# Delta stage: a level's transposes and the next level's first product put into one step

## The chip, the cores and the metric

One core of one Trainium2 chip runs the kernel. The metric is the device time of one execution in microseconds (us). A figure for a kernel is the median of several executions. Besides these, one execution was taken by the hardware profiler. Its span, from the first to the last instruction, and its own rows are what the argument below works with. TensorE multiplies matrices, VectorE (DVE in the rows), ScalarE (ACT) and GpSimd (POOL) do the element-wise work, and SyncE (SP) issues the DMAs.

## The reference, cut to what matters

The model has two layers. The first has a gated delta rule as its mixer, the second an attention. The change touches the delta rule alone, here for one head, with chunks of 64 tokens:

```
L = where(strict, (k*beta) @ k.T * decay, 0)            # per chunk, 64 x 64
u, w = solve(I + L, [v*beta, k*beta*exp(g)])            # unit lower triangular
for each chunk:
    v_new = u - w @ state
    o     = (q*exp(g)) @ state + a_qk @ v_new
    state = state * exp(g_last) + (k*exp(g_last - g)).T @ v_new
o = rms_norm(o, norm_g) * silu(z)
```

q, k, v and z come from a projection of the input (1024 tokens by 1024 features), a causal convolution with four taps and a SiLU; q and k are normalized. There are 8 heads of 128 columns.

## The kernel before, in words

`delta_net` runs 9 iterations (`it` = 0 to 8) of 64 steps (`s` = 0 to 63). The order of all work is written out by hand: every engine has a loop over the same steps and does in each step what is placed there, in order, and semaphores alone tie the engines together. An engine that reaches a step early goes on until a wait holds it.

In iteration `it` TensorE projects head `it`: each step has three matmuls of 128x512 columns (`project`, L424 to L426). Behind the three come the pieces of the head before, `p = it - 1` (`head_work`). So iterations 1 to 7 have both, iteration 0 has no head work, and iteration 8 has no projection; there `keep_warm` (L465) issues one dummy matmul in each step from `AT_CHUNKS` on.

The pieces of head work on TensorE, in order of steps before the change:

- step 1 and 2: the products k k (L486) and k q (L490); step 3, 8 and 9: transposes (`turn`, L475) of k, of the first inverse `inv` and of v.
- steps 11 to 28, the levels: `(I + L)` is inverted by doubling blocks in 6 levels of three steps. The first step of a level is the product y (L526, in the last level L522), which DVE masks (L848, L844). The second is the product x (L546, L541), which DVE adds into `inv_t` (L861, L857). The third has the four transposes of `inv_t` (L475), which ACT copies to `inv` (L717). The last level has no transposes, so step 28 is empty.
- steps 29 to 52, the chunks: 8 pairs of chunks of three steps each, one for each matmul that waits for DVE: L560 waits for the state (L873), L566 for the rest (L866), L570 for v_new (L870).
- step 59: the column sums of the squared output (`column_sums`, L470, here "the second sums").

Head `it` has work of its own in the same iteration, at fixed steps: DVE convolves it in the odd steps from 9 to 55 (`convolve`, L787 for the first tap and L789 for the others; six half tensors of four taps). ACT takes each projected half out of PSUM in every eighth step (L620, L613), applies SiLU at step 41 (up to L660), and TensorE makes the column sums of the squared k at step 45 (L470, "the first sums"). ACT turns those into a norm (L645 to L649). Then come, on ACT, the half of step 48 (L620), the squares of q (L668, step 51), the high part of the next weights (L604, step 52), the second half of the output (L728) and its square (L729, step 53). On POOL come the normalization of k (L402, step 49), the low part of those weights (L391, step 52) and the sum of the two squares of the output (L405, step 53), for which the second sums wait. At step 59 ACT turns the second sums into a norm, DVE applies it (L831, step 62) and goes on to the next head's triangular matrix and its first inverse (L814 to L825), for which the transposes of step 8 wait. In iteration 7 there are no more weights to split, so L604 and L391 of step 52 are absent.

`keep_warm` and the wait of the second sums look like this:

```
rounds = int(s >= AT_CHUNKS)
...
pe.wait_ge(norms, p + 2)
pe.wait_ge(o_added, p + 1)
column_sums((w0[:, 0:HALF], w0[:, HALF:T]), eg, o_summed)
```

Of the kernel before, what the change touches and what calls it, by code (L numbers as in the profile page):

```python
# [15 lines left out]
NT = T // P  # L16
# [8 lines left out]
LEVELS = 6  # L25
# [202 lines left out]
AT_FIRST = 8  # L228
AT_VALUES = 9
AT_LEVELS = 11  # L230
AT_CHUNKS = 29
AT_O_TAKE = 41
AT_SILU = 41
AT_K_SUMS = 45
# [15 lines left out]
def delta_net(nc, c, ring, ahead, after, xh, xl, gates, w_in, gate_bias, a_log_dram, conv_w, norm_g, g_rows_dram, qkvz_space, o_t):  # L250
    with Phase(nc, "gdn") as ph:
# [8 lines left out]
        inv, inv_t = sb("inv", [P, T // 2]), sb("inv_t", [P, T // 2])  # L260
# [22 lines left out]
        w0, w1, w2 = ps("w0", [P, T]), ps("w1", [P, T]), ps("w2", [P, T])  # L283
# [13 lines left out]
        k_turned, kd_made = sem("k_turned"), sem("kd_made")  # L297
        kk_made, qk_made, att_made = sem("kk_made"), sem("qk_made"), sem("att_made")
        q_decayed, inv2_made, inv2_turned, inv2_copied = sem("q_decayed"), sem("inv2_made"), sem("inv2_turned"), sem("inv2_copied")
        y_product, y_made, x_product, x_made = sem("y_product"), sem("y_made"), sem("x_product"), sem("x_made")  # L300
        t_turned, t_copied = sem("t_turned"), sem("t_copied")
# [112 lines left out]
        def _(pe):  # L414
# [58 lines left out]
            def turn(out, src, signal, chunks):  # L473
                for n in chunks:
                    mm = pe.transpose(out[:, chunk(n)], src[:, chunk(n)], c["ident"][:])  # L475
                mm.then_inc(signal, 1)

            def head_work(p, s):
                q, k, v = (qkvz[:, p % 2, n] for n in range(3))
                if s == AT_KK:  # L480
                    pe.wait_ge(normed, p + 1)
                    if p:

                        pe.wait_ge(s_made, 9 * p)
                    for n in range(NT):
                        mm = pe.matmul(w2[:, chunk(n)], k[:, chunk(n)], k[:, chunk(n)], start=True, stop=True)  # L486
                    mm.then_inc(kk_made, 1)
                if s == AT_QK:
                    for n in range(NT):
                        mm = pe.matmul(w1[:, chunk(n)], k[:, chunk(n)], q[:, chunk(n)], start=True, stop=True)  # L490
                    mm.then_inc(qk_made, 1)
                if s == AT_FIRST:
                    pe.wait_ge(inv2_made, p + 1)
                    turn(w2, inv, inv2_turned, range(NT // 2))
                if s == AT_KEYS:
                    if p:

                        pe.wait_ge(o_rms, p)
                    turn(w0, k, k_turned, range(NT))
                if s == AT_VALUES:  # L500
                    pe.wait_ge(v_ready, p + 1)
                    pe.wait_ge(att_made, p + 1)
                    turn(w1, v, v_turned, range(NT))
                if s == AT_O_SUMS:
                    if p + 1 < H:

                        pe.wait_ge(norms, p + 2)
                    pe.wait_ge(o_added, p + 1)
                    column_sums((w0[:, 0:HALF], w0[:, HALF:T]), eg, o_summed)
                level, what = (s - AT_LEVELS) // 3, (s - AT_LEVELS) % 3  # L510
                if 0 <= level < LEVELS:
                    last = level == LEVELS - 1
                    if what == 0:
                        if level == 0:
                            pe.wait_ge(inv2_copied, p + 1)
                        else:
                            pe.wait_ge(x_made, LEVELS * p + level)
                        for q2 in range(NT // 2):
                            for m in range(2):
                                n = 2 * q2 + m  # L520
                                if last:
                                    mm = pe.matmul(w2[side(m), place(1, q2, HALF_P)], lower[side(1), own(n, 0)],  # L522
                                                   inv_t[side(1), square(n)], start=True, stop=True)
                                    continue
                                for b in (m, 1 - m):
                                    mm = pe.matmul(as_blocks(w2[side(m), place(b, q2, HALF_P // 2)], level),  # L526
                                                   lower[side(b), own(n, b)],
                                                   right_halves(inv_t[side(b), square(n)], level),
                                                   start=True, stop=True)
                        mm.then_inc(y_product, 1)  # L530
                    if what == 1:
                        pe.wait_ge(y_made, LEVELS * p + level + 1)
                        if level == 0:

                            pe.wait_ge(bv_made, p + 1)
                        else:
                            pe.wait_ge(t_copied, (LEVELS - 1) * p + level)
                        for q2 in range(NT // 2):
                            for m in range(2):
                                if last:  # L540
                                    mm = pe.matmul(w1[side(0), place(m, q2, HALF_P)], inv[side(m), square(2 * q2)],  # L541
                                                   y[side(m), square(q2)], start=True, stop=True)
                                    continue
                                for b in (m, 1 - m):
                                    at = (b * NT // 2 + q2) * HALF_P // 2
                                    mm = pe.matmul(w1[side(b), place(m, q2, HALF_P // 2)], inv[side(m), square(2 * q2 + b)],  # L546
                                                   y[side(m), at:at + HALF_P // 2], start=True, stop=True)
                        mm.then_inc(x_product, 1)
                    if what == 2 and not last:
                        pe.wait_ge(x_made, LEVELS * p + level + 1)  # L550
                        if level == 0:

                            pe.wait_ge(kd_made, p + 1)
                        turn(w0, inv_t, t_turned, range(NT // 2))
                n, what = (s - AT_CHUNKS) // 3, (s - AT_CHUNKS) % 3
                if 0 <= n < NT and s >= AT_CHUNKS:
                    if what == 0:
                        pe.wait_ge(s_made, 9 * p + n + 1)
                        pe.wait_ge(q_decayed, p + 1)
                        pe.matmul(w2[:, 0:P], k[:, chunk(n)], state[:, n % 2], start=True, stop=True).then_inc(ks_made, 1)  # L560
                        pe.matmul(w0[:, chunk(n)], state[:, n % 2], q[:, chunk(n)], start=True, stop=False)
                    if what == 1:
                        pe.wait_ge(x_made, LEVELS * (p + 1))
                        pe.wait_ge(full_made, 2 * p + 2)
                        pe.wait_ge(rest_made, NT * p + n + 1)
                        pe.matmul(w2[:, HALF:HALF + P], full_t[:, chunk(n)], rest[:], start=True, stop=True  # L566
                                  ).then_inc(tr_made, 1)
                    if what == 2:
                        pe.wait_ge(vn_made, NT * p + n + 1)
                        pe.matmul(w1[:, 0:P], k_rows[:, chunk(n)], v_new[:], start=True, stop=True).then_inc(ds_made, 1)  # L570
                        pe.matmul(w0[:, chunk(n)], v_new[:], att_t[:, chunk(n)], start=False, stop=True
                                  ).then_inc(o_made, 1)
# [20 lines left out]
        def _(act):  # L593
# [89 lines left out]
            for it in range(H + 1):  # L683
                p = it - 1
                for s in range(STEPS):
# [22 lines left out]
                    if s == AT_VALUES:  # L708
                        act.wait_ge(v_turned, p + 1)
                        for n in range(NT):  # L710
                            step(act.activation(v_rows[:, chunk(n)], w1[:, chunk(n)], ACT.Copy,
                                                scale=gates["beta"][:, n, p:p + 1]),
                                 bv_made, n == NT - 1)
                    level, what = (s - AT_LEVELS) // 3, (s - AT_LEVELS) % 3
                    if 0 <= level < LEVELS - 1 and what == 2:
                        act.wait_ge(t_turned, (LEVELS - 1) * p + level + 1)
                        step(act.activation(inv[:], w0[:, 0:HALF], ACT.Copy), t_copied)  # L717
                        if level == LEVELS - 2:
                            act.wait_ge(x_made, LEVELS * p + LEVELS - 1)
                            for b in range(2):  # L720
                                step(act.activation(full_t[side(b)].rearrange("p (n two t) -> p n two t", n=NT, two=2)[:, :, b],
                                                    inv_t[side(b)].rearrange("p (n t) -> p n t", n=NT), ACT.Copy), full_made)
# [15 lines left out]
        def _(dve):  # L738
# [69 lines left out]
            def head_work(p, s):  # L808
# [24 lines left out]
                if s == AT_QK:  # L833
# [1 line left out]
                    dve.wait_ge(decays, 2 * p + 2)  # L835
                    step(dve.tensor_tensor(att_t[:, 0:HALF], w1[:, 0:HALF], att_t[:, 0:HALF], ALU.mult))
                    step(dve.tensor_tensor(att_t[:, HALF:T], w1[:, HALF:T], att_t[:, HALF:T], ALU.mult), att_made)
                level, what = (s - AT_LEVELS) // 3, (s - AT_LEVELS) % 3
                if 0 <= level < LEVELS:
                    last = level == LEVELS - 1  # L840
                    if what == 0:
# [1249 lines left out]
```

## Time and profile before

| | us |
|---|---|
| median of 3 executions | 1914.57 |
| lowest, highest | 1911.27, 1914.67 |
| profiled execution, its own time | 1915.8 |
| profiled execution, span | 1912.1 |
| busy in the span: PE, DVE, ACT, POOL | 1770.5, 927.3, 755.9, 238.5 |
| delta stage in the span, about | from 25 to 719 |
| mean granted TensorE clock | 0.973 |

The table is to be read with care for TensorE: its matmuls are pipelined and the ends of them are modelled, so that two matmuls overlap in the rows and a busy engine need not be one at its peak. In the sums below, distances between starts are used wherever that is possible. POOL's share is small, but its single instructions are long.

### The profile page before, as it was taken

The numbers are of one execution on the slowest core, as the hardware profiler recorded it, in microseconds if no ns is written. First come the engines' busy times: TensorE is split into PE (matmuls) and PEld (weight loads), VectorE is DVE, ScalarE is ACT, GpSimd is POOL, SyncE is SP. The second block draws the span as 40 slices with busy tenths as digits, with TensorE's granted clock in tenths as the row PEclk, the third lists the DMA queues.
The fourth block names the chain that finished last, engine by engine and source line by source line (L and its number), as shares of the span: only waits on it lengthen the run. The fifth ranks groups of instructions, "written<-read, shape, count | busy, mean of one in ns | idle before, by whom it ended". The sixth has DMA issues, their size and how long they took to land. (4 is left out here: it accounts for less than half of the span.)

```text
span 1912.1 us, 29101 instructions
## 1 busy us (share of the span) xinstructions
PE 1770.5 (93%) x11308; PEld 1307.7 (68%) x11308; DVE 927.3 (48%) x1748; ACT 755.9 (40%) x1239; POOL 238.5 (12%) x199
## 2 busy tenths in 40 slices
PE   7999999999999779979989999999999999899798
PEld 5777777777777648768777886555555555478587
DVE  3767677676675627553322101334334443465523
ACT  3536455354553514042223213545544554441411
POOL 2212212122121101200000001111111110012000
PEclk9999999999999889989989999999999999989899
DMA  5111011210111005141031102111111101041311
GB/s 135 41 51 34 23 46 19 49 35 23 46 31 37 1 1 166 34 132 42 36 101 45 46 0 56 42 28 39 29 42 28 37 19 39 1 158 40 97 56 47
DMA packets 113799, 92.34 MB, mean 48 GB/s; under 512 B 19776, under 2 KB 95744, under 8 KB 113664
## 3 DMA queue, kind: packets, MB, share of 16 engines
q1 hardware_dynamic: 113664, 90.49, 16.4%
q8 instruction: 90, 1.47, 0.3%
q14 instruction: 45, 0.37, 0.1%
HBM read 81.99 MB, written 8.49 MB: 47 GB/s over the span
## 5 line engine op out<-in xcount | busy, mean ns | idle before, releaser
L424 PE MATMUL gdn_unit<-part_hi,gdn_w_hi 128*128 128x512 f32 x512 | 235.4, 460 | 0.2 <-DVE gdn_w_lo L746 0.2
L426 PE MATMUL gdn_unit<-part_hi,gdn_w_lo 128*128 128x512 f32 x512 | 201.7, 394 | 0.0
L425 PE MATMUL gdn_unit<-part_lo,gdn_w_hi 128*128 128x512 f32 x512 | 200.7, 392 | 0.0
L1954 DVE CUSTOM_DVE_ANT_0 fa_probs<-fa_scores,fa_decay 128x896 f32<-128x896 f32 (+7 forms) x128 | 97.0, 758 | 125.0 <-PE fa_scores L1769 80.5
L1788 PE MATMUL fa_turned<-ident,fa_probs 128*128 128x128 f32 x576 | 102.9, 288 | 32.8 <-ACT fa_probs_t L1903 15.4
L1788 PEld LDWEIGHTS fa_turned<-ident,fa_probs 128*128 128x128 f32 x576 | 61.0, 140 | 104.5 <-issue 52.3
L789 DVE SCALAR_TENSOR_TENSOR x<-gdn_raw,gdn_taps,x 128x512 f32<-128x512 f32 x144 | 123.7, 859 | 5.1
L1903 ACT ACTIVATE fa_probs_t<-fa_turned 128x512 f32<-128x512 f32 (+1 forms) x96 | 52.3, 545 | 181.7 <-PE fa_turned L1788 180.8
L1721 PE MATMUL fa_unit<-part_hi,fa_w_hi 128*128 128x512 f32 x256 | 115.0, 449 | 1.5 <-DVE fa_w_lo L1981 1.5
L426 PEld LDWEIGHTS gdn_unit<-part_hi,gdn_w_lo 128*128 128x128 f32 x512 | 96.1, 188 | 21.5
L1961 DVE COPY fa_probs_t<-fa_turned 128x512 f32<-128x512 f32 (+3 forms) x96 | 47.2, 491 | 127.2 <-PE fa_turned L1788 126.9
L391 POOL TENSOR_TENSOR gdn_w_lo<-ring,gdn_w_hi 128x1024 fp32r<-128x1024 f32 x31 | 75.2, 2424 | 269.0 <-ACT gdn_w_hi L604 269.0
L1897 ACT ACTIVATE fa_probs<-fa_probs,fa_top 128x896 f32<-128x896 f32 (+7 forms) x128 | 99.6, 778 | 20.0 <-DVE fa_top L1954 16.0
L424 PEld LDWEIGHTS gdn_unit<-part_hi,gdn_w_hi 128*128 128x128 f32 x512 | 96.9, 189 | 15.0 <-issue 3.6
L1186 PE MATMUL e_gate<-e_w_hi,e_a_hi 128*128 128x512 f32 x256 | 103.1, 403 | 2.8 <-DVE e_a_lo L1323 2.8
L425 PEld LDWEIGHTS gdn_unit<-part_lo,gdn_w_hi 128*128 128x128 f32 x512 | 97.3, 190 | 10.9 <-issue 3.6
L1723 PE MATMUL fa_unit<-part_hi,fa_w_lo 128*128 128x512 f32 x256 | 101.0, 394 | 0.0
L953 PE MATMUL m_y<-part_hi,m_o_hi 128*128 128x512 f32 x256 | 100.6, 393 | 0.0
L954 PE MATMUL m_y<-part_lo,m_o_hi 128*128 128x512 f32 x256 | 100.2, 391 | 0.0
L1188 PE MATMUL e_gate<-e_w_hi,e_a_lo 128*128 128x512 f32 x256 | 100.1, 391 | 0.0
L955 PE MATMUL m_y<-part_hi,m_o_lo 128*128 128x512 f32 x256 | 100.0, 391 | 0.0
L1722 PE MATMUL fa_unit<-part_lo,fa_w_hi 128*128 128x512 f32 x256 | 100.0, 391 | 0.0
(290 smaller groups left out, 3616.3 us busy)
## 6 DMA issues: line engine op xcount, KB each, us to landing
ring<-in_gdn_w_in_dram SPq DMA_DIRECT2D x32, 512.0 KB, 4.1
ring<-in_ple_w_gate_dram SPq DMA_DIRECT2D x32, 256.0 KB, 3.0
ring<-in_fox_w_in_dram SPq DMA_DIRECT2D x32, 256.0 KB, 3.2
ring<-in_fox_w_in_dram SPq DMA_DIRECT2D x16, 512.0 KB, 4.8
fa_decay<-c_rows_scratch SPq DMA_DIRECT2D x64, 128.0 KB, 3.1
in_x_tile<-in_x_dram SPq DMA_DIRECT2D x8, 512.0 KB, 6.7
gdn_g_bc<-g_rows_scratch SPq DMA_DIRECT2D x8, 512.0 KB, 8.5
m_old<-in_x_dram SPq DMA_DIRECT2D x8, 512.0 KB, 3.6
```

What stands on the lines that cost most here:

```text
L424: pe.matmul(out, w_hi[:, j % 2, k, :], xh[:, k, ts], start=(k == 0), stop=False)
L425: pe.matmul(out, w_hi[:, j % 2, k, :], xl[:, k, ts], start=False, stop=False)
L426: mm = pe.matmul(out, w_lo[:, j % 2, k, :], xh[:, k, ts], start=False, stop=(k == KT - 1))
L789: step(dve.scalar_tensor_tensor(out, shifted, weight, out, ALU.mult, ALU.add), conv_made if part == TAPS - 1 else None)
L953: pe.matmul(y[:, cols], o_hi[:, t % OB, k, :], w_hi[:, k, cols], start=(k == 0), stop=False)
L954: pe.matmul(y[:, cols], o_hi[:, t % OB, k, :], w_lo[:, k, cols], start=False, stop=False)
L955: mm = pe.matmul(y[:, cols], o_lo[:, t % OB, k, :], w_hi[:, k, cols], start=False, stop=(k == KT - 1))
L1186: pe.matmul(out[:, cols], hi, w_hi[:, k, cols], start=first, stop=False)
L1188: mm = pe.matmul(out[:, cols], lo, w_hi[:, k, cols], start=False, stop=end)
L1721: pe.matmul(out, w_hi[:, j % 2, k, :], xh[:, k, ts], start=(k == 0), stop=False)
L1723: mm = pe.matmul(out, w_lo[:, j % 2, k, :], xh[:, k, ts], start=False, stop=(k == KT - 1))
L1788: mm = pe.transpose(turned[:, b * P:(b + 1) * P], probs[:, n % 3, j * P:(j + 1) * P], c["ident"][:])
```

## The change

The levels take two steps instead of three. The four transposes of a level move from the third step of that level to the first step of the next one, ahead of the product y of that level and behind the same wait for `x_made`. ACT's copy moves with them. The chunks begin right behind the levels, so `AT_CHUNKS` falls from 29 to 23, and the chunks end at step 46 instead of 52. All other steps keep their numbers.

```
-AT_CHUNKS = 29
+AT_CHUNKS = AT_LEVELS + 2 * LEVELS
...
-                level, what = (s - AT_LEVELS) // 3, (s - AT_LEVELS) % 3
+                level, what = (s - AT_LEVELS) // 2, (s - AT_LEVELS) % 2
                 if 0 <= level < LEVELS:
                     last = level == LEVELS - 1
                     if what == 0:
...
                         else:
                             pe.wait_ge(x_made, LEVELS * p + level)
+                            if level == 1:
+                                pe.wait_ge(kd_made, p + 1)
+                            turn(w0, inv_t, t_turned, range(NT // 2))
...
-                    if what == 2 and not last:
-                        pe.wait_ge(x_made, LEVELS * p + level + 1)
-                        if level == 0:
-                            pe.wait_ge(kd_made, p + 1)
-                        turn(w0, inv_t, t_turned, range(NT // 2))
...
-                    level, what = (s - AT_LEVELS) // 3, (s - AT_LEVELS) % 3
-                    if 0 <= level < LEVELS - 1 and what == 2:
-                        act.wait_ge(t_turned, (LEVELS - 1) * p + level + 1)
+                    level, what = (s - AT_LEVELS) // 2, (s - AT_LEVELS) % 2
+                    if 0 < level < LEVELS and what == 0:
+                        act.wait_ge(t_turned, (LEVELS - 1) * p + level)
                         step(act.activation(inv[:], w0[:, 0:HALF], ACT.Copy), t_copied)
-                        if level == LEVELS - 2:
+                        if level == LEVELS - 1:
                             act.wait_ge(x_made, LEVELS * p + LEVELS - 1)
...
-                level, what = (s - AT_LEVELS) // 3, (s - AT_LEVELS) % 3
+                level, what = (s - AT_LEVELS) // 2, (s - AT_LEVELS) % 2
```

The first pair of changed lines stands in TensorE's part, the second in ACT's, the last in DVE's.

## Rows read from the trace of the kernel before

**Rows 1.** The page, part 1: busy time, share of the span, instructions.
```profile
PE 1770.5 (93%) x11308; PEld 1307.7 (68%) x11308; DVE 927.3 (48%) x1748; ACT 755.9 (40%) x1239; POOL 238.5 (12%) x199
```

**Rows 2.** The waits of TensorE: total, times, longest.
```profile
PE gdn_w L566 <- DVE gdn_rest L866: 7.2, 8, 1.0
```

**Rows 3.** Timeline of TensorE in the levels of iteration 4: start, length.
```profile
342.03 0.66 PE L475 MATMUL gdn_w<-ident,gdn_inv_t 128*128 128x128 f32 x4
342.44 0.48 PE L424 MATMUL gdn_unit<-part_hi,gdn_w_hi 128*128 128x512 f32 x1
...
343.32 0.67 PE L526 MATMUL gdn_w<-gdn_inv_t,gdn_lower 64*64 64x32 f32 x32
...
346.28 0.66 PE L475 MATMUL gdn_w<-ident,gdn_inv_t 128*128 128x128 f32 x4
```

**Rows 4.** Timeline of TensorE in iteration 8: transposes with a product behind them.
```profile
651.70 1.06 PE L475 MATMUL gdn_w<-ident,x 128*128 128x128 f32 x8 [0.89 <-DVE gdn_att_t L837]
652.69 0.67 PE L526 MATMUL gdn_w<-gdn_inv_t,gdn_lower 64*64 64x32 f32 x32
```

**Rows 5.** Timeline of TensorE in iteration 4: chunks, then steps without head work.
```profile
372.44 0.38 PE L566 MATMUL gdn_w<-gdn_rest,gdn_full_t 128*128 128x128 f32 x2
...
375.69 0.38 PE L566 MATMUL gdn_w<-gdn_rest,gdn_full_t 128*128 128x128 f32 x2
...
393.65 0.39 PE L424 MATMUL gdn_unit<-part_hi,gdn_w_hi 128*128 128x512 f32 x1
...
394.33 0.39 PE L424 MATMUL gdn_unit<-part_hi,gdn_w_hi 128*128 128x512 f32 x1
```

**Rows 6.** Timeline of TensorE: both sums, the next step 8; first sums of iteration 7.
```profile
382.38 1.88 PE L470 MATMUL gdn_w<-gdn_squares,ones 128*128 128x512 f32 x4
...
397.74 1.88 PE L470 MATMUL gdn_w<-gdn_eg,ones 128*128 128x512 f32 x4
...
414.04 0.66 PE L475 MATMUL gdn_w<-ident,gdn_inv 128*128 128x128 f32 x4 [1.05 <-DVE gdn_inv L825]
...
619.17 1.88 PE L470 MATMUL gdn_w<-gdn_squares,ones 128*128 128x512 f32 x4
```

**Rows 7.** Timeline of ScalarE in iteration 4: copy in a level; output's square.
```profile
347.03 0.60 ACT L717 ACTIVATE gdn_inv<-gdn_w 128x512 f32<-128x512 f32 x1 [1.47 <-PE gdn_w L475]
...
393.85 1.07 ACT L729 ACTIVATE gdn_eg<-o_t 128x1024 f32<-128x1024 f32 x1
```

**Rows 8.** Timeline of GpSimd in iteration 4, between the sums.
```profile
388.29 2.39 POOL L402 TENSOR_TENSOR x<-x,gdn_squares 128x1024 f32<-128x1024 f32 x1 [17.82 <-ACT gdn_squares L649]
391.13 2.37 POOL L391 TENSOR_TENSOR gdn_w_lo<-ring,gdn_w_hi 128x1024 fp32r<-128x1024 f32 x1 [0.45 <-ACT gdn_w_hi L604]
395.06 2.43 POOL L405 TENSOR_TENSOR gdn_eg<-gdn_eg,o_t 128x1024 f32<-128x1024 f32 x1 [1.55 <-ACT gdn_eg L729]
```

**Rows 9.** Timeline of VectorE: a convolution held, one alone, the norm applied.
```profile
388.92 2.05 DVE L787 TENSOR_SCALAR x<-gdn_raw,gdn_taps 128x512 f32<-128x512 f32 x1
...
394.47 0.75 DVE L789 SCALAR_TENSOR_TENSOR x<-gdn_raw,gdn_taps,x 128x512 f32<-128x512 f32 x1
...
403.59 1.28 DVE L831 SCALAR_TENSOR_TENSOR o_t<-o_t,gdn_gain,gdn_eg 128x1024 f32<-128x1024 f32 x1 [1.10 <-ACT gdn_eg L649]
```

**Rows 10.** Timeline of iteration 0, steps 51 to 53: GpSimd, then VectorE.
```profile
81.22 2.89 POOL L391 TENSOR_TENSOR gdn_w_lo<-ring,gdn_w_hi 128x1024 fp32r<-128x1024 f32 x1 [0.44 <-ACT gdn_w_hi L604]
...
81.11 3.55 DVE L789 SCALAR_TENSOR_TENSOR x<-gdn_raw,gdn_taps,x 128x512 f32<-128x512 f32 x2
```

**Rows 11.** Timeline of iteration 8: the second sums of the last head.
```profile
706.71 2.34 POOL L405 TENSOR_TENSOR gdn_eg<-gdn_eg,gdn_squares 128x1024 f32<-128x1024 f32 x1 [60.07 <-ACT gdn_eg L729]
709.11 1.98 PE L470 MATMUL gdn_w<-gdn_eg,ones 128*128 128x512 f32 x4 [2.71 <-POOL gdn_eg L405]
```

**Rows 12.** Timeline of ScalarE in iteration 7: the squares of q.
```profile
627.56 1.06 ACT L668 ACTIVATE gdn_squares<-x 128x1024 f32<-128x1024 f32 x1 [1.99 <-POOL x L402]
```

**Rows 13.** Windows, part of iteration 8: busy time of each engine, granted clock, DMA.
```profile
650.00:680.00 30.00, 19.30 (x385) 15.71 (x386) 7.97 (x26) 7.42 (x18) 0.00 (x0) 0.61 0.01 2
```

## The prediction

> **What bounds the kernel now.** I read the page first: TensorE is busy for 1770.5 of 1912.1 us, no other engine for half of the span [rows 1]. So the kernel looks bound by TensorE, and a change of order could bring only the waits that remain, or the cost of switching between kinds of work. TensorE's waits come next: inside the delta stage the largest one that the change can touch is L566 for DVE's rest, 7.2 us over 8 heads, 1.0 at most [rows 2]. Then I went through the timelines of iteration 4, engine by engine, since all iterations from 1 to 7 repeat it within a few hundredths. They show what the shares hide: the iteration has a second bound, almost as long as TensorE. From the second sums (397.74) to the transposes of the next step 8 (414.04) are 16.30 us, and they end in a wait of 1.05 us for DVE [rows 6]. That stretch is a chain: sums, the norm on ACT, DVE's gain, triangle and inverse. It hangs on the start of the second sums, not on TensorE. And the second sums themselves start at 397.74, where POOL's sum of squares ended at 395.06 + 2.43 = 397.49 [rows 6, 8]: TensorE came 0.2 us after its operand. Whoever moves TensorE ahead of that operand gains nothing.
>
> So I cut an iteration at three places: step 8 to the first sums, first to second sums (397.74 - 382.38 = 15.36 us), second sums to the next step 8 (16.30 us).
>
> **Step 8 to the first sums gets longer.** The first sums stay at step 45. Before the change the levels, the empty step 28, five chunks and the first two steps of the sixth lie ahead of them. After it, seven chunks and two steps of the eighth do. The number of projection steps between is the same. A plain step takes 394.33 - 393.65 = 0.68 us, a chunk of three steps 375.69 - 372.44 = 3.25 [rows 5], so the head work of one chunk costs 3.25 - 3 x 0.68 = 1.21 and the two that move ahead of the sums 2.42 us.
>
> What the merged step saves is small. Before, a product y starts 343.32 - 342.03 = 1.29 us behind its transposes, with a projection between them; four transposes take 342.44 - 342.03 = 0.41, or 0.10 each [rows 3]. Where a product follows transposes directly, it starts 652.69 - 651.70 = 0.99 behind eight of them [rows 4], 0.17 more than their 8 x 0.103 = 0.82. After the change it should start 0.41 + 0.17 = 0.58 behind four, and the displaced projection runs elsewhere for 0.68: 1.26 against 1.29. That is 0.03 us for a level, 0.15 for the five of a head. The bounds: nothing, and 1.29 - 0.41 - 0.68 = 0.20 a level, 1.0 a head, if the product could follow at once. I take 0.15, as the row of the same pair of instructions says.
>
> The waits inside the levels stay. The transposes wait for the same add with the same one projection between. The product x now has one projection and one product between it and the transposes, that is 0.58 and about the 1.29 + 0.2 that a product and a projection fill now, together 2.1 us. ACT's copy ends 347.03 + 0.60 - 346.28 = 1.35 behind the start of the transposes [rows 3, 7], so 0.7 covers it; with that cover gone the product would wait in each level by what the copy is late. On ACT the high part of step 20 now stands behind the copy of step 19, once a head; the next copy comes over 3 us later, room enough for it. No moved step issues a DMA. SP's loads follow POOL's low parts, and on SP's and POOL's queues nothing is reordered. The steps from 39 to 45, in which ACT makes the squares for the first sums, are chunk steps before and after, so their margin stays. The sum for this part is 2.42 - 0.15 = +2.27 us.
>
> **First to second sums.** TensorE alone would need less: 15.36 less the two chunks (2.42) less the wait of 1.0 [rows 2], which vanishes since L566 no longer runs at step 51, behind the convolution that POOL holds [rows 9]. That is 11.94 us. But the operand of the second sums is not ready by then. Counted from the start of the first sums (382.38):
>
> - POOL's normalization of k ends at 388.29 + 2.39 = 390.68, at 8.30. Nothing before it changes.
> - POOL's low part waits for ACT's high part and starts at 391.13, at 8.75 [rows 8]. Nothing before it changes either.
> - Before the change DVE had a chunk's rest to do there, and the low part took 2.37. Now DVE comes out of the held convolution at 388.92 + 2.05 = 390.97 [rows 9] and goes straight into the next. Iteration 0, which has no head work, shows just that order: a convolution at 81.11, the low part at 81.22, and the latter takes 2.89 instead of 2.37 [rows 8, 10]. So it ends at 8.75 + 2.89 = 11.64.
> - In iteration 0 the next convolution waits for the low part's end at 81.22 + 2.89 = 84.11 and ends itself at 81.11 + 3.55 = 84.66, 0.55 later [rows 10]. In the new order POOL's sum of squares is ready to go at that moment: its operand, which before came last (393.85 + 1.07 = 394.92 [rows 7]), is now made right behind the high part, as the chunks have ended long before. The convolution already waits, so I let it go first: 11.64 + 0.55 = 12.19.
> - The sum of squares takes 2.34 undisturbed [rows 11]: 14.5.
>
> The second sums therefore start 14.5 us after the first, 2.6 after TensorE is there. The stretch shrinks by 0.86 instead of 3.4. The lower bound of these terms is that DVE and POOL do not hold each other in the new places: 8.75 + 2.37 + 2.43 and 0.1 for starts make 13.65 [rows 8]. The upper one is that each waits for the whole of the other: the convolution of step 51 and that of step 53, 0.75 each alone [rows 9], then 8.6 (390.97) + 0.75 + 2.37 + 0.75 + 2.34 = 14.8.
>
> The Trainium skill's page SBUF — State Buffer, section "Who interferes with whom", says that a DVE instruction with two SBUF inputs and a GpSimd instruction that reads SBUF exclude each other for the whole instruction, whichever was issued first. The row of iteration 0 agrees in direction; by the rule in full it would be the upper bound, 0.3 us a head more and 1926 us in all, by the rows 1924.5.
>
> **Second sums to the next step 8.** The chain stays 16.30. A sums group that starts from a wait took 1.98 instead of 1.88 [rows 6, 11], so +0.1. On DVE sixteen decay instructions and a last convolution follow the sum of squares, before as after, since POOL holds the first of them. They end at 403.59 - 1.10 = 402.49, 1.1 ahead of the norm [rows 9]; without the 0.2 that the sums were late that is 0.9. Were they later, DVE would take the norm up later by as much.
>
> **The sum.** Per head in iterations 1 to 6: 2.27 + (14.5 - 15.36) + 0.1 = +1.51, six times +9.1. In iteration 7 there is no low part at step 52, but ACT's squares of q wait for POOL and end at 627.56 + 1.06 = 628.62 [rows 12]; the output's second half (0.60), its square (1.06) and POOL's sum (2.43) with their starts bring the second sums to 13.8 after 619.17 [rows 6]: 2.27 + 13.8 - 15.36 + 0.1 = +0.8. Iteration 0 has no head work: 0. In iteration 8 the same instructions follow in the same order with no projection between; six more dummy matmuls run behind the chunks (6 x 0.23 = 1.4 us), inside a wait of 2.71 for POOL [rows 11], whose chain they do not touch: 0. Were that wait gone, they would cost 1.4. In all +9.9 us. The profiled execution would go from 1915.8 (span 1912.1) to 1925.7. It lay 1.2 above the median of 1914.57, so for the median I predict **1924.5 us**.
>
> **The rivals.**
>
> - *The port waits do not come, the chain does.* 2.27 + 13.65 - 15.36 + 0.1 = +0.66 a head, seven times +4.6: 1919.2. For it: POOL's sum might be issued before the waiting convolution. Against it: 2.89 in rows 10.
> - *The merged step saves all of the switching*, 1.0 a head instead of 0.15: 9.9 - 7 x 0.85 = +4.0, 1918.5. For it: the projection behind transposes starts at once. Against it: the 0.99 of rows 4, one case only.
> - *The other side: TensorE keeps its pace.* If the operand of the second sums is there after 11.9 us, each head gains the wait and the saving, 1.0 + 0.15, seven times is -8.1: 1906.5. The point that decides is the distance from first to second sums: below 15.36 - 2.27 - 0.1 = 13.0 us the change gains, above it loses. For it: TensorE met no wait for that operand in iterations 1 to 7. Against it: the low part and the sum of squares alone fill 8.75 to 13.5.
> - *The new stall lets TensorE's clock fall.* In iteration 8, where wait follows wait, the mean granted clock was 0.61 over 30 us [rows 13], so part of it at 1.2 GHz. If 3 us of work per head ran at half speed, 7 x 1.5 = 10.5 more: 1935. Against it: after the lone wait of 2.71 the sums took 1.98, so the clock held at 2.4 GHz [rows 11]. The Trainium skill's page TensorE: Matmul & The Clock Gate, section "HAM oscillation — how this bites in real kernels", warns that idle gaps bring the half clock back; no row here shows it for a lone gap of this size.
>
> **How the numbers follow.** The forecast gets 0.60, the missing port waits 0.15, the full saving 0.08, the fallen clock 0.07, TensorE's pace 0.10. The range leaves out the last two and little of the rest: from 1917 (the lower cases together, with some noise) to 1930 (upper bound of the port, 1926, nothing saved by merging, 1 more, and the spread of 3 us between executions). About 0.2% or 4 us is what a measurement of this kernel can tell from no change. The forecast and the clock are slower, 0.67, of the missing port waits 0.10 and of the full saving 0.03: slower 0.80. The rest of these two is 0.10 for within 0.2%. Faster is 0.10.
>
> **What the profile of the changed kernel would show.** First, a wait of PE L470 for POOL L405 in seven more heads, of about 2.6 us. Second, L566's wait for the rest down from 8 times to 1. Third, L391 of step 52 at about 2.9 us and L405 about 2.7. Fourth, first to second sums 14.5 apart, and each iteration from 1 to 6 longer by 1.5. Fifth, L526 0.58 behind the transposes. The prediction is wrong if the sums lie under 13 us apart, if the transposes or the product x meet a new wait in the levels, or if the granted clock falls inside iterations 1 to 7.

## The result and the profile after

The changed kernel takes 1931.36 us in the median of 4 executions (1929.43 to 1932.70), the kernel before 1914.09 in the median of 4 (the fourth, 1913.61, joined the three that the forecast started from). The ratio is 1.0092 with a 95% interval of 1.0075 to 1.011: slower by 17 us. The forecast was 1924.5 with a range up to 1930, so the direction was right and the size was not.

The waits of TensorE in the profiled execution (span 1927.3), as in [rows 2]: total, times, longest.

```profile
PE gdn_w L470 <- POOL gdn_eg L405: 19.2, 8, 2.7
...
PE gdn_w L564 <- DVE gdn_rest L864: 0.2, 1, 0.2
```

The wait for the rest is gone but for 0.2 (7.2 us before), and a wait of the second sums for POOL, which only iteration 8 had, now comes in each of the eight heads. The rows of TensorE in iteration 4 answer to [rows 3, 6]: a level, both sums, the next step 8.

```profile
348.25 0.66 PE L475 MATMUL gdn_w<-ident,gdn_inv_t 128*128 128x128 f32 x4
348.84 0.67 PE L530 MATMUL gdn_w<-gdn_inv_t,gdn_lower 64*64 64x32 f32 x32
...
351.80 0.66 PE L475 MATMUL gdn_w<-ident,gdn_inv_t 128*128 128x128 f32 x4
...
391.24 1.88 PE L470 MATMUL gdn_w<-gdn_squares,ones 128*128 128x512 f32 x4
...
405.78 3.58 PE L470 MATMUL gdn_w<-gdn_eg,ones 128*128 128x512 f32 x4 [2.64 <-POOL gdn_eg L405]
...
423.79 0.66 PE L475 MATMUL gdn_w<-ident,gdn_inv 128*128 128x128 f32 x4 [1.06 <-DVE gdn_inv L823]
```

The product stands 0.59 behind its transposes (0.58 forecast), and a level takes 3.55 instead of 4.25. From first to second sums are 14.54 (14.5 forecast), with a wait of 2.64 (2.6 forecast). The new thing is the length of the second sums: 3.58 instead of 1.88. GpSimd between the sums, as in [rows 8], then VectorE:

```profile
399.99 2.90 POOL L391 TENSOR_TENSOR gdn_w_lo<-ring,gdn_w_hi 128x1024 fp32r<-128x1024 f32 x1 [0.44 <-ACT gdn_w_hi L602]
402.85 2.79 POOL L405 TENSOR_TENSOR gdn_eg<-gdn_eg,o_t 128x1024 f32<-128x1024 f32 x1
```
```profile
399.87 3.56 DVE L787 SCALAR_TENSOR_TENSOR x<-gdn_raw,gdn_taps,x 128x512 f32<-128x512 f32 x2
```

The low part grew from 2.37 to 2.90 and the sum of squares from 2.43 to 2.79: both start while a convolution runs, and they follow each other with no gap. That is the chain as forecast. The windows of the second sums in iterations 1, 3 and 4 show what the forecast lacked. The columns are the busy times and counts of PE, its weight loads, DVE, ACT and POOL, then the granted clock, the DMA share and GB/s.

```profile
161.60:163.60 2.00, 1.92 (x5) 0.99 (x6) 1.96 (x9) 0.00 (x0) 0.00 (x0) 1.00 0.00 0
...
323.20:326.20 3.00, 2.90 (x5) 1.31 (x5) 2.96 (x12) 0.00 (x0) 0.00 (x0) 0.59 0.00 0
405.70:408.70 3.00, 2.92 (x5) 1.40 (x5) 2.96 (x12) 0.00 (x0) 0.00 (x0) 0.50 0.00 0
```

In iterations 3 to 6 the clock fell to 1.2 GHz (0.50) behind the wait; the 0.59 of iteration 3 is the mean of a stretch in which it fell only after the sums had begun. In 1, 2 and 7 it stayed at 2.4 GHz, and the sums took 1.95. At 1.2 GHz they take 3.35 to 3.58 instead, and since the chain to the next step 8 begins with them, that stretch is 17.8 to 18.1 in those four iterations and 16.4 in 1 and 2.

### The profile page after: what moved, and what is told of

Read it like the earlier page. It is cut to its first block and busy times, and to the rows that moved or that the text cites. A ratio compares the mean times of both kernels' runs of the same rounds, so it can differ in the third digit from the quotient of the medians.

```text
span 1927.3 us, 29113 instructions
## 1 busy us (share of the span) xinstructions
PE 1780.0 (92%) x11314; PEld 1315.3 (68%) x11314; DVE 929.6 (48%) x1748; ACT 754.8 (39%) x1239; POOL 244.0 (13%) x199
## 5 line engine op out<-in xcount | busy, mean ns | idle before, releaser
L1185 PE MATMUL e_gate<-e_w_lo,e_a_hi 128*128 128x512 f32 x256 | 99.8, 390 | 0.0
```

Source lines behind the costliest of these rows:

```text
L1185: pe.matmul(out[:, cols], hi, w_lo[:, k, cols], start=False, stop=False)
```

## The experiments

The theory going in: the loss is made where the chunks move ahead of the first sums while POOL's chain holds the second ones, and by the clock that falls in the wait. The main rival: the merged step itself costs. The first four kernels ran on one chip with the kernel before (1913.44 us there), the next four likewise (1913.48), the last two too (1913.04). The table has iteration 4 of each, from starts in the timelines; the ratios go by the kernel before on the same chip, while a difference between two changed kernels in the text is one of medians from different chips.

| | median us | ratio (95%) | step 8 to first sums | first to second | second to step 8 |
|---|---|---|---|---|---|
| before | 1914.09 | | 47.25 | 15.36 | 16.30 |
| forecast for after | 1924.5 | | 49.5 | 14.5 | 16.4 |
| after | 1931.36 | 1.0092 (1.0075 to 1.011) | 49.89 | 14.54 | 18.01 |
| e1 merged steps alone | 1912.88 | 0.9996 (0.9986 to 1.0005) | 47.17 | 15.38 | 16.32 |
| e2 chunks from 26 | 1914.74 | 1.0011 (1.0001 to 1.002) | 48.39 | 14.57 | 16.38 |
| e3 dummy matmuls | 1921.92 | 1.0047 (1.0032 to 1.0062) | 49.89 | 14.50 | 16.41 |
| e4 split late | 1917.76 | 1.0021 (1.0012 to 1.003) | 51.50 | 11.90 | 17.44 |
| e5 split late, decays early | 1914.39 | 1.0004 (0.9995 to 1.0013) | 49.86 | 12.01 | 16.38 |
| e6 before, split late | 1912.66 | 1.0 (0.9991 to 1.001) | 47.22 | 15.37 | 16.29 |
| e7 decays early | 1923.82 | 1.006 (1.0045 to 1.0076) | 49.86 | 13.84 | 16.39 |
| e8 sum on TensorE | 1914.45 | 1.0007 (0.9998 to 1.0016) | 49.85 | 11.79 | 17.99 |
| e9 all together | 1905.70 | 0.9956 (0.9942 to 0.997) | 49.89 | 11.99 | 16.39 |
| e10 without the buffer | 1908.19 | 0.997 (0.9959 to 0.9982) | 49.89 | 12.02 | 16.39 |

**e1: the merged steps alone.** The changed kernel with the chunks back at step 29.

```
-AT_CHUNKS = AT_LEVELS + 2 * LEVELS
+AT_CHUNKS = 29
```

> One part of the change alone: the merged steps stay, the chunks begin at step 29 again. Chain theory (the loss comes from moving chunks ahead of the first sums while POOL's chain holds the second sums, and from the stall that follows): step 8 to first sums about 47.1, first to second sums 15.4, no long wait before the second sums, so 1913 us, within 0.2% of the kernel before. Rival (the merged step itself costs, by transposes and product back to back): most of the 17 us stays, 1925 us or more.

Measured: 1912.88 us, no difference from before. The rival falls: transposes and product back to back neither cost nor save anything that the median can tell. Step 8 to first sums went from 47.25 to 47.17 in iteration 4, 0.08 where I had forecast 0.15. Over the seven heads even that is gone (331.2 us against 331.1), since in iterations 2 and 7 a new wait of 0.3 comes in the levels (below). So all of the loss hangs on the place of the chunks.

**e2: half of the move.** `AT_CHUNKS = 26`.

> Half of the move: merged steps, chunks from step 26. Chain theory: step 8 to first sums +1.1, first to second sums 14.5 as in the changed kernel, since POOL's chain sets it; TensorE waits about 1.4 us for it and its clock does not fall: +0.3 a head, 1916 us. Rival (any wait there lets the clock fall): slow sums of 3.4 us in some heads, 1922 us or more. Rival (time goes with the number of chunks moved): half of the 17 us, 1922 us.

Measured: 1914.74 us, 1.3 above before, of an expected 2 to 3. First to second sums is 14.57, the same as with the whole move; TensorE waits 1.4 us for POOL there, and no sums are slow. So the loss does not go with the number of chunks moved. The first three steps cost next to nothing in the median, the second three the other 16 us, of which about 9 are the clock (e3). Next to nothing is flattering, though: iterations 1 to 7 of the profiled execution take 3.15 us more than before (555.32 against 552.17), and the code behind the stage takes less, for a reason that stays open (below).

**e3: dummy matmuls in the wait.** They read loaded weights and write a bank that nobody reads at that point.

```
+                    if p + 1 < H:
+                        for n in range(10):
+                            pe.matmul(w2[:, 0:HALF], w_hi[:, 1, 0, :], xh[:, 0, 0:HALF], start=True, stop=True)
                     pe.wait_ge(o_added, p + 1)
```

> The changed kernel with ten dummy matmuls (2.3 us) in front of the second sums' wait, into a bank that nobody reads. Clock theory: the second sums take 1.9 us in every head, second sums to step 8 is 16.4 in all of them, first to second sums stays 14.5; 4 heads times 1.6 us come back: 1925 us. Rival (slow sums have another cause, such as the idle wait's length on POOL or DVE): no change, 1931 us.

TensorE in iteration 4 of e3, the ten dummies and the second sums:

```profile
401.15 2.43 PE L510 MATMUL gdn_w<-part_hi,gdn_w_hi 128*128 128x512 f32 x10
403.90 1.98 PE L470 MATMUL gdn_w<-gdn_eg,ones 128*128 128x512 f32 x4 [0.33 <-POOL gdn_eg L405]
```

Measured: 1921.92 us, 9.4 less than the changed kernel, where 6.4 were expected. Each taken against the kernel before on its own chip (+17.3 and +8.5), the difference is 8.8. The sums take 1.98 or less in iterations 1 to 7, and 16.4 follow in 1 to 6. POOL's operand comes as late as ever (14.50). Only the clock is different, so this is what the fallen clock costs. The profile of the changed kernel has four slow heads of 1.5 to 1.7 us, 6.3 in all; the 9 in the medians speak for more of them in the other executions. The mean granted clock agrees: 0.972 in the profiled execution, which was the fastest of the four, and 0.968 to 0.969 in the other three, against 0.974 to 0.975 in e3. How many heads were slow there, no trace shows.

**e4: the split of the next weights late.** ACT's high part and POOL's low part of step 52 go behind POOL's sum of squares (step 54).

```
+AT_SPLITS = (4, 20, 36, 54)
...
-                    if it < H and s % 16 == 4 and 4 * it + s // 16 + 1 < 4 * H:
+                    if it < H and s in AT_SPLITS and 4 * it + s // 16 + 1 < 4 * H:
```

> The changed kernel with the split of the next weights (ACT's high part, POOL's low part) of step 52 moved behind POOL's sum of squares. Chain theory: the sum of squares starts some 9.4 us after the first sums and ends at 12.0 to 12.4, the second sums at 12.1 to 12.5 with hardly a wait, no clock fall; but the low part then holds DVE's decay instructions, and the norm is applied 1.7 us later than its operand is there: second sums to step 8 about 18.0. Together 1920 us. Rival (the second sums are held by something else than the low part, by ACT or DVE): first to second sums stays at 14.5, 1931 us or more.

GpSimd in iteration 4 of e4, where the sums start at 388.58 and 400.48:

```profile
397.93 2.40 POOL L406 TENSOR_TENSOR gdn_eg<-gdn_eg,o_t 128x1024 f32<-128x1024 f32 x1 [1.04 <-ACT gdn_eg L728]
400.41 2.69 POOL L392 TENSOR_TENSOR gdn_w_lo<-ring,gdn_w_hi 128x1024 fp32r<-128x1024 f32 x1
```

Measured: 1917.76 us, 13.6 less than the changed kernel (11 expected), 13.0 against the kernels before of the same chips. With the low part out of the way, the second sums start 11.90 after the first, without a wait: the chain was what held them. But the low part now stops DVE's decay instructions, the norm waits for DVE, and the wait for the inverse grows to 2.1 in six heads. In three of them the clock fell behind it: step 8 to first sums took 51.2 to 51.5 there (iteration 4 of the table is one of them) and 49.6 to 49.9 in the rest. It fell once more behind the wait of 2.07 in iteration 7, where there is no split to move and the second sums come 13.95 after the first, as in the changed kernel.

**e6: the late split in the kernel before.**

> The kernel before with the split of step 52 behind POOL's sum of squares, nothing else. Chain theory: first to second sums stays near 15.2, since there the chunks and not the low part come last; the low part runs from about 15.1 to 17.6 after the first sums and makes DVE's decays late, so second sums to step 8 is up to 1.4 longer: 1914 to 1924 us, no gain. Rival (the late split is good by itself): 1908 us.

Measured: 1912.66 us and the same three stretches as before. The late split is no gain by itself. The longer last stretch that I allowed for did not come either.

**e7: the decays early.** In the changed kernel, `AT_DECAYS = 47` instead of 55, which is possible only since the chunks end at step 46: the decays of the second kind wait for the last chunk.

> The changed kernel with DVE's decay instructions at step 47 alone, the split stays at step 52. Chain theory: POOL's low part is still ahead of its sum of squares; it meets no convolution at its start, only short decay instructions, so first to second sums falls from 14.5 to about 14.1, with a wait of 2.2 and clock falls in some heads: 1926 to 1929 us. Rival (DVE's lateness is what costs): 1915 us or less.

Measured: 1923.82 us, a little under the forecast; first to second sums is 13.7 to 13.8 in iterations 1 to 6, with waits of 1.8 to 1.9 and no slow sums in the profiled execution. That was the fastest of four (1920.08, granted clock 0.974; the others 1922.76 to 1925.99 at 0.970 to 0.972). DVE's lateness is not what costs most, as the rival had it: that would have brought 1915 or less.

**e8: POOL's sum taken away.**

```
-                        step(pool.tensor_tensor(eg[:], eg[:], q_squares(p), ALU.add), o_added)
...
+                        pe.matmul(w0[:, ts], c["ones"][:], q_squares(p)[:, ts], start=True, stop=False)
+                        mm = pe.matmul(w0[:, ts], c["ones"][:], eg[:, ts], start=False, stop=True)
```

> The changed kernel without POOL's sum of squares: TensorE adds the two squares itself, with four instead of two matmuls in the second sums. Chain theory: the second sums start when TensorE comes, 11.9 after the first, without a wait; they take 1.3 longer, so the norm starts 1.3 earlier than in the changed kernel with full clock; the clock does not fall: 7 x (1.3 + about 1.3) less than 1931, 1913 us. Rival (the low part or ACT holds the second sums, not POOL's sum): 14 or more from first to second sums, 1925 us or more.

Measured: 1914.45 us, 1.5 above the forecast and level with the kernel before. The sums start when TensorE comes, 11.79 after the first; they are 1.6 longer (1.3 expected), and the stretch behind them is 18.0. Both POOL instructions were needed for the 14.5: with either of them out of the way (e4, e8), the second sums do not wait in iterations 1 to 6.

**e5: late split and early decays.**

> The changed kernel with the split of step 52 behind POOL's sum of squares, and with DVE's decay instructions moved from step 55 to step 47, so that the low part cannot make them late. Chain theory: first to second sums 12.0, second sums to step 8 again 16.4 with a wait of 1.1 for the inverse (17.4 and 2.1 with the late split alone), no wait over 1.5 us and so no clock fall: 0.9 us a head under the kernel before, 1907 us, faster by 0.3%. Rival (DVE is full: its convolutions behind the decays are now late, and the norm waits for them): second sums to step 8 stays at 17.4 or more, 1914 us or more.

Measured: 1914.39 us, 7 above the forecast, although iterations 1 to 6 came out as expected: 12.0 and 16.4. The miss was in two places that the expectation had not looked at. The first is the first inverse of the first head, as the decays go ahead of the convolution's steps 47 to 53 in iteration 0 too:

```profile
102.75 1.11 PE L476 MATMUL gdn_w<-ident,gdn_inv 128*128 128x128 f32 x4 [3.23 <-DVE gdn_inv L824]
```

It came 28.1 after the first sums instead of 25.6, and behind that wait of 3.23 the clock fell: 1.11 for four transposes instead of 0.66. e7 has the same (28.11, a wait of 3.22, 1.12). The second is iteration 7, where first to second sums was 14.28 instead of 12.0. Most of that is no price of the edit: ACT's squares of q wait for POOL's normalization there, as in the changed kernel, which has 13.95 in iteration 7. The early decays add the other 0.33, in e7 too (14.29). Together the two places make 5.7 of the 7 us: 2.5 and 0.9 in the first, 2.3 in the second.

**e9 and e10: the late split, and the decays early in iterations 1 to 6 only.** e9 also puts the last head's squares of q into a part of the convolution's input that is free by then, so that ACT need not wait for POOL (`normed`); e10 does without that.

```
-                if s == AT_DECAYS:
+                if s == (AT_DECAYS_EARLY if 1 <= h < H - 1 else AT_DECAYS):
...
-            return o_t[:, h + 1] if h + 1 < H else squares[:]
+            return o_t[:, h + 1] if h + 1 < H else raw[:, 0, TAPS - 1:]
```

> The changed kernel with the late split, with the decays at step 47 in iterations 1 to 6 only (at step 55 in 0 and 7), and with the last head's squares of q in the free half of the convolution's input, so that ACT need not wait for POOL there. Chain theory: iteration 0 as before (25.6 from first sums to step 8), iterations 1 to 6 at 49.8 + 12.0 + 16.4 = 78.2 against 79.0, iteration 7 first to second sums 12 to 12.5 against 15.4, no clock fall inside iterations 1 to 7: about 6 us under the kernel before, 1907 us. Rival (the rest of the kernel or iteration 8 takes it back, or DVE is late in iteration 7): 1912 us or more.

> The same without the other place for the last head's squares: ACT waits for POOL's normalization in iteration 7, first to second sums 14.0 there with a wait of 2.1. Chain theory: 2 us more than with it, perhaps a fallen clock once: 1909 to 1911 us.

TensorE's wait for POOL's sum in e9, the total over the span; it is that of iteration 8 alone:

```profile
PE gdn_w L472 <- POOL gdn_eg L407: 1.4, 1, 1.4
```

Both sums and the next step 8 in iteration 4, then GpSimd between and behind the sums (e9):

```profile
382.92 1.88 PE L472 MATMUL gdn_w<-gdn_squares,ones 128*128 128x512 f32 x4
...
394.91 1.95 PE L472 MATMUL gdn_w<-gdn_eg,ones 128*128 128x512 f32 x4
...
411.30 0.66 PE L477 MATMUL gdn_w<-ident,gdn_inv 128*128 128x128 f32 x4 [1.05 <-DVE gdn_inv L822]
```
```profile
392.28 2.48 POOL L407 TENSOR_TENSOR gdn_eg<-gdn_eg,o_t 128x1024 f32<-128x1024 f32 x1 [0.98 <-ACT gdn_eg L726]
394.85 2.35 POOL L393 TENSOR_TENSOR gdn_w_lo<-ring,gdn_w_hi 128x1024 fp32r<-128x1024 f32 x1
```

Measured: e9 1905.70 us, 0.44% faster than the kernel before and 1.3% than the changed one; e10 1908.19, 2.5 more. POOL's sum of squares ends at 392.28 + 2.48 = 394.76, and the second sums start at 394.91: the operand is there just as TensorE comes. An iteration takes 49.89 + 11.99 + 16.39 = 78.27 against 78.91 before, 78.0 where the first stretch is 49.6. Iterations 1 to 7 take 6.0 us less than in the kernel before (546.2 against 552.2); some 3 us more are gained behind the delta stage, for the open reason below, and iteration 8 is 0.8 longer. In iteration 7 first to second sums is 11.9 in e9. In e10 it is 13.94, with a wait of 2.04 and sums of 2.78 instead of 1.96: there the clock fell once.

## Why the prediction was wrong in size

**The step that failed: the sum took TensorE's clock as holding behind the new stall.** It gave the second sums +0.1 a head, as they start from a wait; in four of seven heads they and the chain behind them took 1.5 to 1.7 us more than that. I had seen this as a rival, *the new stall lets TensorE's clock fall*, and set it at 0.07, on the ground that after the lone wait of 2.71 the sums took 1.98 [rows 11]. That was one case, and it carried too much. In e6, whose iteration 8 has the same instructions as the kernel before, the same wait came out the other way:

```profile
708.84 3.78 PE L471 MATMUL gdn_w<-gdn_eg,ones 128*128 128x512 f32 x4 [2.72 <-POOL gdn_eg L406]
```

In the changed kernel the clock fell in 4 of 7 heads for 6.3 us in the profiled execution, and e3 gives it about 9 us in the medians. The price that I had given the rival, 10.5 us, was about right; its chance rested on too little. With the forecast's 9.9 it makes 20, with the profiled share 16. The Trainium skill, TensorE: Matmul & The Clock Gate, section "HAM oscillation — how this bites in real kernels", warns of idle gaps in a matmul stream. The trace agrees in direction, in four of the seven heads, and for waits of 2.64 us, which are shorter than the gaps that the section describes.

Point by point:

- **Step 8 to the first sums:** forecast +2.27, measured 49.6 to 49.95 against 47.24 to 47.54, which is +2.47 in the mean of the seven heads. (That the iterations repeat within a few hundredths holds for the other two stretches; this one varies by 0.3 before the change as well.) The two chunks are about as sized. The merging gave 0.08 in an undisturbed head (e1), not 0.15. In four of the seven heads 0.3 is lost, in three different places. In iterations 2 and 7 the product x waits for DVE's y in a level (L550, 0.29 and 0.27 us). No kernel with levels of three steps has that there, and every one with merged steps does, e1 too, so this is a small price of the merged step. The prediction had looked at ACT's copy only, and had named a new wait of the product x as a sign of being wrong. The totals over the span, before and after:

```profile
PE gdn_w L546 <- DVE gdn_y L848: 3.2, 4, 0.8
```
```profile
PE gdn_w L550 <- DVE gdn_y L846: 3.8, 6, 0.8
```

In iteration 3 the wait for the state is 0.9 instead of 0.6, as in the kernel before. In iteration 4 the 0.3 is lost in the last chunk ahead of the first sums; its cause is open.
- **First to second sums:** forecast 14.5, measured 14.54, with the low part at 2.90 (2.89 forecast) and the sum of squares at 2.79 (about 2.7 forecast). In iteration 7 forecast 13.8, measured 13.95. Iteration 0, which ran without head work, did show the order in which DVE and POOL hold each other. By the Trainium skill's page SBUF — State Buffer, section "Who interferes with whom", in full, I had an upper bound of 14.8; the 14.54 lie below it, so the rows again came out at less than the whole instruction. e4 and e8 show that the two POOL instructions in a row are the cause, and e7 that the convolutions' part in it is under 1 us: with decays in their place it is 13.65 to 13.84.
- **Second sums to step 8:** forecast 16.4, measured 16.37 and 16.38 where the clock held, and 17.8 to 18.1 where it fell.
- **Iteration 8:** forecast 0. It took 59.67 from step 8 to the second sums instead of 58.95, but e6 has 59.66 in the unchanged order and e3 58.93 in the changed one, so this is scatter. It goes with the clock: the granted mean over that stretch is 0.77 in the kernel before and in e3, 0.74 in the changed kernel and in e6. The dummies were covered: the wait fell from 2.71 to 1.34.
- **The sum:** iterations 1 to 7 of the profiled execution took 17.6 us more. Without the 6.3 of the clock that is 11.3, where 9.9 was forecast, and the +2.47 instead of +2.27 a head is what is left. Behind the last head's second sums, in code that is the same, the profiled execution was 2.7 shorter than that of before. That repeats: the three profiled kernels with the chunks from step 29 (before, e1, e6) take 1202.5 to 1204.9 us there, the nine others 1199.2 to 1200.9. Part of it is one wait of TensorE at the start of a later part of the kernel, 3.9 to 4.6 in the three and 2.5 to 2.6 in the nine. Before and after:

```profile
PE fv_bank L122 <- PEq L49: 4.6, 1, 4.6
```
```profile
PE fv_bank L122 <- PEq L49: 2.5, 1, 2.5
```

Its cause is open, and no term of the prediction has it. So it is partly luck that e3, where the clock holds, is only 8.5 us above the kernel before and near the forecast of 9.9: in iterations 1 to 7 it loses 11.2, and the code behind them gives some 3 back.

The rivals "the port waits do not come" and "the merged step saves all of the switching" are refuted by the 14.54 and by e1. "TensorE keeps its pace" failed at its own point of decision: 14.54 lies above 13.0. In e4 the distance is 11.9 and yet no gain is left, since the delay went on to DVE's decays: the point was right for this chain and left out the next one.

## What to carry to other kernels

A step that frees time on the busiest engine is worth what the next chain leaves of it. Here two pieces of work fixed at step numbers (the sums at 45 and 59) were left where they were while the work around them moved, and the order on a nearly idle engine, POOL at 13%, decided the result. After such a move, look at what is queued ahead of the last operand, on every engine, and move that too: the same change loses 0.9% alone and gains 0.4% once the split, the decays and the last head's squares of q are placed anew (e9). And a wait of TensorE should be priced with its clock: one row where the clock held is no proof.

## What the runs showed of the hardware

- Waits of TensorE in iterations 1 to 7 and the clock behind them: of the 13 waits for POOL from 0.9 to 1.9 us in e2 and e7 none had slow work behind it, nor had the waits of 0.5 to 1.1 us for the inverse in any kernel. Of 17 waits from 2.0 to 2.7 us (after, e4, e5, e7, e10) nine had, in the same kernel now one way and now the other, and so had both of 3.2 us (e5, e7). A fall cost 1.5 to 1.7 us in each of the four heads of the changed kernel, and 0.6 to 1.6 in e4 and e10.
- In e3 ten dummy matmuls, 2.43 us together, stand in front of the wait. The clock held in all seven heads, and the second sums started no later (14.50 against 14.54 behind the first).
- A GpSimd instruction of 2.4 us that started under a running VectorE convolution took 2.8 to 2.9 (after, e8), and the convolution behind that one ended only after it: 3.56 us for two that take 0.75 each alone.
- Four transposes directly followed by a product on a quarter of the array cost as much, within 0.1 us a head, as with a projection between them (e1).
